# A two-branch decoder step on one core: row sums on TensorE, a first product moved inside PSUM, GpSimd work in pieces

## The chip, the cores and the metric

The kernel runs on one core of a Trainium2 chip. Its time is device time in microseconds (us), the median of several runs on the chip. A core has TensorE (PE) for matrix products, VectorE (DVE), ScalarE (ACT) and GpSimd (POOL) for elementwise work, SyncE (SP) and the DMA queues for transfers. Operands lie in SBUF; TensorE writes its products to PSUM, eight banks of which the other engines read and write.

## The reference

One step of a decoder layer for 1024 prompt rows and 8 sample rows, width 1024, in float32. A mixer comes first, then a squared-ReLU feed-forward block of width 4096:

```python
def trunk(x, c, ...):
    mod = (silu(c) @ w_ada[l] + b_ada[l])[:, None, :]
    sh1, sc1, g1, sh2, sc2, g2 = jnp.split(mod, N_MOD, axis=-1)
    h = rmsnorm(x, norm1_g[l]) * (1 + sc1) + sh1
    y, bp, bs, bc = mixer(h, ...)            # input projection, convolutions, output projection
    x = x + g1 * y
    h = rmsnorm(x, norm2_g[l]) * (1 + sc2) + sh2
    x = x + g2 * (jnp.square(jax.nn.relu(h @ w_ff1[l])) @ w_ff2[l])
    return rmsnorm(x, final_g), ...
```

The change lies in the last of these blocks: the entry to `h @ w_ff1` with the root mean square of x that it needs, and the product with `w_ff2`.

## The kernel before

**Numbers.** A float32 operand is split into a rounded high half and a low half (value minus high half). A product is high by high, high by low and low by high: three matmuls. ScalarE makes high halves (`high_split`, L1043, of weights; `queue_high`, L1109, of hidden tiles), VectorE or GpSimd makes low halves by a subtraction (VectorE: `low_split` L1779 and `queue_low` L1892; GpSimd: `low_split` L825, four blocks of 128x1024 or the last one 128x512).

**Seven products.** The feed-forward weights and the activations are cut in 2x2 blocks and multiplied by a Strassen-Winograd scheme: products p0 to p6 in place of eight. Sums of weight blocks are made by VectorE's `mix_weights` (L1763 to L1769, four additions of 128x512), sums of hidden tiles by `mix_hidden` (L1829 to L1836). While a product's bank in PSUM is still to be read by another engine, TensorE can't start the next product in that bank.

**Up-projection (`h @ w_ff1`).** Sixteen units; each has seven products of 24 matmuls of 128x262 (L2335, from `product_of`, or `up` in unit 0). Bank pairs are `BANK_X[unit % 2]` for p0, p2, p4 and p6, `BANK_Y` for p1 and `BANK_V` for p3 and p5. ScalarE copies three partial results of a unit from PSUM (`copy_c`, L1094), VectorE adds the rest (`add_c`, L1793; `last_c`, L1816), scales by the row norms (`scale_c`), ScalarE applies ReLU and square (`activate`, L1101 and L1104), SyncE stores the hidden tiles to memory (`store_hidden`) and later fetches the queue pieces back.

The norm of x's rows is needed only at `scale_c`. Squares are made in place, a tile of 128x1024 at a time (`square_row`, L1026); VectorE adds rows 0 to 6 onto row 7 (`add_row`, L1842); TensorE sums over the partitions with a column of ones (`hidden_sums`, which calls `token_sums`, L2138, 16 matmuls of one column), and spreads the norm over a bank (`hidden_spread`, L2391 to L2396). All of it lies in units 0 and 1, the entry of the up-projection. Its order is written out by hand, per engine; ScalarE's copy after the squares waits for `rows_summed`.

**Product stage (with `w_ff2`).** Fourteen rounds w of 14 steps. A step is product p of output block jj, 12 matmuls of 128x258 (L2444, `down(w, n)`), in the order of `STEPS`. After each step VectorE's `gather` (L1942 where the sum is touched first, L1945 afterwards) adds the bank pair to the sum in SBUF, and `y_added` counts these additions; a step waits until the addition that read its bank is counted. Between the additions VectorE has, by the round, four `mix_weights` and a number of `queue_low`. ScalarE makes the high halves of the next round's weights and of the next group's queue pieces (two rounds share a group). Four weight blocks a round get their low half from GpSimd. `QUEUE` is the order of the queue pieces. After the last round come `rejoin` and `part`, which finish the output.

```python
STEPS = [(0, 0), (0, 1), (1, 0), (3, 0), (2, 0), (2, 1), (1, 1), (5, 0), (4, 0), (4, 1), (3, 1), (6, 0), (6, 1), (5, 1)]
bank = (BANK_X[jj], BANK_Y, BANK_X[jj], BANK_V, BANK_X[jj], BANK_V, BANK_X[jj])[p]
```

## Time and profile before

| | us |
|---|---|
| median of three runs | 1103.91 (1102.61 to 1107.77) |
| the profiled execution: its own time | 1106.11 |
| span of its profile | 1104.3 |
| TensorE busy | 1038.8 |
| VectorE busy | 902.8 |
| ScalarE busy | 407.5 |
| GpSimd busy | 241.9 |

The profile shows one execution. Times within it are microseconds from the start of the span. A row of a group gives busy time and mean ns of one instruction; idle time before an instruction is put down to the event that ended it last. PEld is TensorE's loading of weights, which runs beside its matmuls. The mean granted TensorE clock was 0.979 of full speed.

### The profile page before, as it was taken

To read this page: it belongs to the slowest core of one execution; us is meant where nothing else is said; L and a number is where in the kernel's file an instruction comes from. 1 tells how busy PE (TensorE), PEld (TensorE's weight loads), DVE (VectorE), ACT (ScalarE), POOL (GpSimd) and SP (SyncE) were. 2 spreads that over 40 slices of the span, in tenths; PEclk is the share of its full clock that TensorE was granted. 3 is DMA by queue.
4 is the path that set the end of the run, shared out by engine and by line. 5 is a ranking of instruction groups with operands and counts; after the bars stand their busy time and mean duration, and the time that the engine had idled before them with its cause. 6 is when DMAs were issued, how large, how long until landed. Compare 5 with 4: busy or idle time off the path is not lost.

```text
span 1104.3 us, 19181 instructions
## 1 busy us (share of the span) xinstructions
PE 1038.8 (94%) x7811; PEld 1003.2 (91%) x7811; DVE 902.8 (82%) x1236; ACT 407.5 (37%) x584; POOL 241.9 (22%) x188
## 2 busy tenths in 40 slices
PE   7899999999999769899999999998999999998896
PEld 5688898999999669799999999988999999998896
DVE  5799899996458986677677677699999999998866
ACT  6321111111233554555555455472333333332221
POOL 2741121221114200000000000033443443443300
PEclk8899999999999989999999999999999999999999
DMA  9967411110113130544534534585554444335212
GB/s 279 352 235 299 138 39 39 39 42 26 48 44 132 77 98 29 188 151 146 165 117 146 174 110 150 184 291 170 148 148 132 144 147 137 98 105 184 78 57 98
DMA packets 112769, 148.62 MB, mean 135 GB/s; under 512 B 6465, under 2 KB 78088, under 8 KB 110617
## 3 DMA queue, kind: packets, MB, share of 16 engines
q1 hardware_dynamic: 111928, 146.15, 41.0%
q8 instruction: 62, 1.02, 0.4%
q0 software_dynamic: 336, 0.58, 0.2%
q10 hardware_dynamic: 417, 0.65, 0.2%
q14 instruction: 26, 0.21, 0.1%
HBM read 110.40 MB, written 37.44 MB: 134 GB/s over the span
## 4 chain that ended last, share of the span: by engine, by line
PE 64%; DVE 21%; issue 9%; DMA 3%; ACT 2%; SPq 1%; DVEq 0%; ACTq 0%
PE banks L2335 25%; PE banks L2107 17%; PE banks L2444 13%; DVE plain L1428 4%; DVE xT L1945 3%; PE banks L2485 3%; DVE split L1892 2%; DMA plain<-hid_home 1%; DVE split L1642 1%; DMA plain<-in_x_prompt 1%; DVE plain L1769 1%; PE banks L2202 1%; PE banks L2224 1%; DVE plain L1447 1%; PE banks L2515 1%
## 5 line engine op out<-in xcount | busy, mean ns | idle before, releaser
L2335 PE MATMUL banks<-split 128*128 128x262 f32 x2688 | 334.2, 287 | 19.3 <-ACT xT L1094 12.1
L2335 PEld LDWEIGHTS banks<-split 128*128 128x128 f32 x2688 | 331.3, 191 | 22.0 <-ACT xT L1094 12.7
L2444 PE MATMUL banks<-split 128*128 128x258 f32 x2352 | 289.3, 285 | 13.0 <-DVE xT L1945 10.9
L2444 PEld LDWEIGHTS banks<-split 128*128 128x128 f32 x2352 | 285.2, 190 | 16.9 <-DVE xT L1945 13.9
L2107 PEld LDWEIGHTS banks<-split 128*128 128x128 f32 x1656 | 265.9, 192 | 12.6 <-issue 7.4
L2107 PE MATMUL banks<-split 128*128 128x344 f32 x1656 | 270.1, 325 | 6.5 <-DVE gate_s L1488 6.0
L825 POOL TENSOR_TENSOR split<-plain,split 128x1024 fp32r<-128x1024 f32 (+1 forms) x59 | 130.3, 2219 | 525.0 <-ACT split L1043 524.9
L1043 ACT ACTIVATE split<-plain 128x1024 fp32r<-128x1024 f32 (+1 forms) x120 | 112.6, 949 | 177.6 <-PE banks L2444 139.4
L1945 DVE TENSOR_TENSOR xT<-xT,banks 128x516 f32<-128x516 f32 x180 | 122.1, 684 | 19.7 <-PE banks L2444 13.8
L1428 DVE SCALAR_TENSOR_TENSOR plain<-plain 128x1023 f32<-128x1023 f32 (+14 forms) x90 | 132.6, 1473 | 2.9
L768 POOL TENSOR_TENSOR split<-plain,split 128x1024 fp32r<-128x1024 f32 (+2 forms) x29 | 64.3, 2218 | 249.0 <-ACT split L876 249.0
L1892 DVE TENSOR_TENSOR split<-plain,split 128x524 fp32r<-128x524 f32 x106 | 113.3, 1074 | 1.1 <-ACT split L1109 1.1
L876 ACT ACTIVATE split<-plain 128x1024 fp32r<-128x1024 f32 (+2 forms) x29 | 27.3, 942 | 210.5 <-PE banks L2107 177.4
L1793 DVE TENSOR_TENSOR xT<-xT,banks 128x524 f32<-128x524 f32 x44 | 30.7, 699 | 54.2 <-PE banks L2335 54.1
L1779 DVE TENSOR_TENSOR split<-plain,split 128x1024 fp32r<-128x1024 f32 (+1 forms) x61 | 66.3, 1087 | 1.9 <-ACT split L1043 1.8
L1109 ACT ACTIVATE split<-plain 128x524 fp32r<-128x524 f32 x106 | 60.5, 628 | 16.8 <-PE banks L2444 12.7
L1101 ACT ACTIVATE xT<-xT 128x516 f32<-128x516 f32 x60 | 43.4, 724 | 49.4 <-DVE xT L1805 49.4
L1094 ACT ACTIVATE xT<-banks 128x524 f32<-128x524 f32 x45 | 27.3, 607 | 69.9 <-PE banks L2335 62.0
L2485 PE MATMUL banks<-split 128*128 128x258 f32 x384 | 49.5, 286 | 3.1 <-DVE gate_s L1999 3.1
L2485 PEld LDWEIGHTS banks<-split 128*128 128x128 f32 x384 | 46.9, 189 | 3.9 <-DVE gate_s L1999 3.9
L1104 ACT ACTIVATE xT<-xT 128x516 f32<-128x516 f32 x60 | 38.2, 637 | 1.9
L1484 DVE SCALAR_TENSOR_TENSOR xT<-banks,modT,xT 128x688 f32<-128x688 f32 x16 | 14.9, 929 | 27.7 <-PE banks L2107 27.7
(233 smaller groups left out, 815.9 us busy)
## 6 DMA issues: line engine op xcount, KB each, us to landing
plain<-hid_home SPq DMA_DIRECT2D x106, 262.0 KB, 3.7
hid_home<-xT SPq DMA_DIRECT2D x102, 262.0 KB, 3.1
plain<-in_w_ff SPq DMA_DIRECT2D x18, 1024.0 KB, 6.6
plain<-in_w_ada SPq DMA_DIRECT2D x16, 1024.0 KB, 7.4
plain<-in_w_ff SPq DMA_DIRECT2D x56, 256.0 KB, 3.7
plain<-in_w_in SPq DMA_DIRECT2D x17, 512.0 KB, 6.2
plain<-in_w_ada SPq DMA_DIRECT2D x16, 512.0 KB, 6.7
plain<-in_x_prompt SPq DMA_DIRECT2D x8, 512.0 KB, 8.2
```

Of the source, the lines that this page charges most:

```text
L768: nc.gpsimd.tensor_tensor(o, a, b, ALU.subtract).then_inc(wlo_ready, 1)
L825: nc.gpsimd.tensor_tensor(split_of(g, 1), split_source(unit, g), split_of(g, 0).bitcast(F32), ALU.subtract).then_inc(split_lo, 1)
L1043: nc.scalar.activation(split_of(g, 0), src, ACT.Copy).then_inc(split_hi, 1)
L1109: nc.scalar.activation(queue_piece(n, 0), stage(n), ACT.Copy).then_inc(queue_hi, 1)
L1428: ins = nc.vector.scalar_tensor_tensor(dc[:, c, s:T], glu[:, c, 0:T - s], tapT[:, tap:tap + 1], dc[:, c, s:T], ALU.mult, ALU.add)
L1779: nc.vector.tensor_tensor(split_of(g, 1), src, split_of(g, 0).bitcast(F32), ALU.subtract).then_inc(split_lo, 1)
L1892: nc.vector.tensor_tensor(queue_piece(n, 1), stage(n), queue_piece(n, 0).bitcast(F32), ALU.subtract).then_inc(queue_lo, 1)
L1945: nc.vector.tensor_tensor(out, out, ps, ALU.add).then_inc(y_added, 1)
L2107: last = nc.tensor.matmul(out[:, t, 0:TW], w[:, slot, b, :], x[:, k, t * TW:(t + 1) * TW], start=(i == 0 and w is whi and x is hi), stop=( ...
L2335: last = nc.tensor.matmul(banks[:, bank + t, 0:width], weight(p, w, i), operand(p, x, pieces[n], t, width), start=(p in FIRST_OF_CHAIN and ...
L2444: last = nc.tensor.matmul(banks[:, bank + t, 0:QT], weight(p, h, 2 * kb + jj), halves(queue_piece(e, x))[:, t, 0:QT], start=(p in FIRST_OF ...
L2485: last = nc.tensor.matmul(banks[:, bank, 0:QT], late_split(j, w)[:, 2 * b + dd, :], src, start=(b == 0 and w == 0 and x == 0), stop=(b == ...
```

## The change

Three edits.

**1. GpSimd in pieces.** Its subtractions of weight low halves (`low_split` and the late ones before the tail) are issued as pieces of 128x512, two where there was one of 128x1024.

**2. Rows 0 and 1 summed by TensorE.** ScalarE squares rows 0 and 1 right after the second weight rounding of unit 0. TensorE sums each over the partitions into a bank that is free then, VectorE reads the result into `sumsq`, scaled, and the norm's formula takes it as an addend. `add_row` has five rows left. In units 0 to 2 the orders of ScalarE and VectorE are written anew; on TensorE `hidden_sums` now stands between p0 and p1 of unit 1 and the two `hidden_spread` after p2 and p3; `mix_hidden(0)` stands ahead of `last_c(1)`.

**3. Product 0 moved inside PSUM.** `STEPS` gets another order. Product 0 of a block is copied by ScalarE from `BANK_X[jj]` to `BANK_Y` (`move`), and product 1 is accumulated onto it, so that VectorE adds 12 bank pairs a round instead of 14. The queue pieces and their halves follow in another order, with some of the first group's made later.

```diff
-STEPS = [(0, 0), (0, 1), (1, 0), (3, 0), (2, 0), (2, 1), (1, 1), (5, 0), (4, 0), (4, 1), (3, 1), (6, 0), (6, 1), (5, 1)]
+STEPS = [(0, 0), (3, 0), (0, 1), (1, 0), (2, 0), (5, 0), (1, 1), (2, 1), (4, 0), (3, 1), (4, 1), (6, 0), (5, 1), (6, 1)]
...
+ADDS = [n for n, (p, _) in enumerate(STEPS) if p]
...
-ROW_SQUARED = {7: 1, 0: 2, 1: 3, 2: 4, 3: 5, 4: 6, 5: 7, 6: 8}
-QUEUE = [(g, p, kb) for g in range(GROUPS) for p in ((0, 1, 2, 3, 4, 5, 6) if g == 0 else (3, 4, 5, 6, 0, 2, 1))
+ROW_SQUARED = {0: 1, 1: 2, 2: 3, 7: 4, 3: 5, 4: 6, 5: 7, 6: 8}
+QUEUE = [(g, p, kb) for g in range(GROUPS) for p in ((0, 1, 2, 3, 4, 5, 6) if g == 0 else (3, 4, 5, 6, 0, 1, 2))
          for kb in range(2)] + [(GROUPS, b, half) for half in range(2) for b in range(FG)]
...
+                out, src, hi = split_of(g, 1), split_source(unit, g), split_of(g, 0).bitcast(F32)
+                for b in range(0, HALF_N[g] // P, 4):
+                    ins = nc.gpsimd.tensor_tensor(out[:, b:b + 4], src[:, b:b + 4], hi[:, b:b + 4], ALU.subtract)
+                ins.then_inc(split_lo, 1)
...
             oper_high(1, 5)
             high_split(0, 1)
+            square_row(0)
+            square_row(1)
...
-            square_row(7)
-            square_row(0)
-            square_row(1)
-            act.wait_ge(rows_summed, 2)
+            act.wait_ge(two_summed, 1)
             copy_c(0, 2, BANK_X[0], 2)
             square_row(2)
             copy_c(0, 1, BANK_V, 3)
+            square_row(7)
+            square_row(3)
             high_split(1, 0)
+            square_row(4)
             high_split(1, 1)
-            square_row(3)
+            square_row(5)
+            square_row(6)
             high_split(1, 2)
-            square_row(4)
-            act.wait_ge(rows_summed, 3)
+            act.wait_ge(rows_summed, 1)
             copy_c(0, 3, BANK_X[0], 6)
             high_split(1, 3)
-            square_row(5)
-            square_row(6)
 
 
             copy_c(1, 0, BANK_X[1], 0)
+            root(3)
             high_split(2, 0)
-            act.wait_ge(rows_summed, 4)
+            act.wait_ge(rows_summed, 2)
             copy_c(1, 2, BANK_X[1], 2)
...
+            def move(w, jj):
+
+                act.wait_ge(product_made, made(UP + 2 * w + jj, 0))
+                if jj:
+                    act.wait_ge(y_added, added_step(w, STEP_AT[1, 0]))
+                elif w:
+                    act.wait_ge(y_added, added_step(w - 1, STEP_AT[1, 1]))
+                else:
+                    act.wait_ge(c_added, added_at(UP - 1, 1))
+                nc.scalar.activation(banks[:, BANK_Y:BANK_Y + 2, 0:QT], banks[:, BANK_X[jj]:BANK_X[jj] + 2, 0:QT],
+                                     ACT.Copy).then_inc(moved, 1)
...
             for g in range(GROUPS):
                 unit, n = UP + 2 * g, 2 * NP * (g + 1)
-                for k in range(4):
-                    queue_high(n + k)
+                move(2 * g, 0)
+                if g:
+                    queue_high(n)
+                    queue_high(n + 1)
+                    queue_high(n + 2)
+                move(2 * g, 1)
+                if g:
+                    queue_high(n + 3)
                 high_split(unit + 1, 0)
-                for k in range(4, 7):
+                for k in range(4 if g else 0, 7 if g else 4):
                     queue_high(n + k)
                 high_split(unit + 1, 1)
-                queue_high(n + 7)
+                if g:
+                    queue_high(n + 7)
                 high_split(unit + 1, 2)
                 high_split(unit + 1, 3)
+                move(2 * g + 1, 0)
+                if g == 0:
+                    queue_high(n + 4)
+                    queue_high(n + 5)
+                    queue_high(n + 6)
...
-            add_row(0, 1)
-            add_row(1, 2)
+            dve.wait_ge(two_summed, 1)
+            nc.vector.tensor_scalar(sumsq[:, 0:KD], banks[:, BANK_X[1] + 1, 0:KD], 1.0 / D, EPS, ALU.mult, ALU.add
+                                    ).then_inc(two_read, 1)
+            add_row(2, 1)
+            add_row(3, 2)
             dve.wait_ge(oper_lo, len(LO_ORDER))
             dve.wait_ge(ext_ready, 3)
             nc.vector.memset(rb[:, :, 0, 256:HT], 1.0).then_inc(rb_ones, 1)
             nc.vector.memset(rb[:, :, 1, 256:258], 1.0).then_inc(rb_ones, 1)
+            add_c(0, 1, BANK_X[0], 4, 2)
+            low_split(1, 0)
+            add_row(4, 3)
             mix_all(1)
-            low_split(1, 0)
-            add_c(0, 1, BANK_X[0], 4, 2)
-            add_row(2, 3)
+            add_c(0, 2, BANK_V, 5, 3)
             low_split(1, 1)
-            add_c(0, 2, BANK_V, 5, 3)
-            add_row(3, 4)
+            add_row(5, 4)
+            add_row(6, 5)
             low_split(1, 2)
-            add_row(4, 5)
             low_split(1, 3)
-            add_row(5, 6)
-            add_row(6, 7)
...
+            dve.wait_ge(sq_used, 2)
+            dve.wait_ge(two_read, 1)
+            link(nc.vector.scalar_tensor_tensor(rstd[:, 0:KD], banks[:, BANK_X[0], 0:KD], 1.0 / D, sumsq[:, 0:KD],
+                                                ALU.mult, ALU.add))
+            nc.vector.tensor_scalar(rstd[0:S, KD:R], banks[0:S, BANK_X[0], KD:R], 1.0 / D, EPS, ALU.mult, ALU.add
+                                    ).then_inc(ms_ready, 1)
+            dve.wait_ge(rows_summed, 5)
+            diagonals(3, diag2)
             add_c(1, 0, BANK_Y, 1, 1)
             mix_all(2)
-            dve.wait_ge(sq_used, 2)
-            mean_squares(3, banks[:, BANK_X[0], :], D)
             low_split(2, 0)
-            dve.wait_ge(rows_summed, 7)
-            diagonals(3, diag2)
-            add_c(1, 1, BANK_X[1], 4, 2)
-            low_split(2, 1)
-            add_c(1, 2, BANK_V, 5, 3)
-            low_split(2, 2)
             dve.wait_ge(rb_ready, 3)
             dve.wait_ge(copied, 4)
             scale_c(0, 0)
             scale_c(0, 1)
             scale_c(0, 2)
+            add_c(1, 1, BANK_X[1], 4, 2)
             scale_c(0, 3)
+            low_split(2, 1)
             scale_c(1, 0)
+            add_c(1, 2, BANK_V, 5, 3)
             scale_c(1, 1)
             scale_c(1, 2)
+            low_split(2, 2)
+            mix_hidden(0)
             last_c(1)
             low_split(2, 3)
-            mix_hidden(0)
...
-                    gather(w, k)
+                    if STEPS[k][0]:
+                        gather(w, k)
...
-                        if k < 2:
-                            queue_low(12 + k)
-                        elif k < 4:
-                            queue_low(n + k - 2)
-                        else:
-                            queue_low(n + k - 6)
+                        queue_low(8 + k if k < 4 else 4 + k)
+                    elif w == 1:
+                        queue_low(n + (4 + k if k < 4 else k))
...
+            pe.wait_ge(row_squared, 2)
+            token_sums(banks[:, x1 + 1, :], xT[:, 0, :], True, False)
+            token_sums(banks[:, x1 + 1, :], xT[:, 1, :], False, True).then_inc(two_summed, 1)
...
+                if unit == 1:
+                    pe.wait_ge(two_read, 1)
                 if unit > 1:
                     pe.wait_ge(c_added, added_at(unit - 2, 4))
                     if unit == 2:
                         pe.wait_ge(rb_ready, 3)
                 product_of(0, x, every, both, every, HT).then_inc(product_made, 1)
+                if unit == 1:
+                    hidden_sums()
                 pe.wait_ge(c_added, added_at(unit - 1, 1))
                 product_of(1, BANK_Y, every, both, every, HT).then_inc(product_made, 1)
-                if unit == 1:
-                    hidden_sums()
                 pe.wait_ge(copied, ahead + 1)
                 pe.wait_ge(split_lo, split_at(unit, 1))
                 product_of(2, x, every, both, every, HT).then_inc(product_made, 1)
+                if unit == 1:
+                    hidden_spread(True)
                 pe.wait_ge(c_added, added_at(unit - 1, 3))
                 product_of(3, BANK_V, every, both, every, HT).then_inc(product_made, 1)
+                if unit == 1:
+                    hidden_spread(False)
                 pe.wait_ge(copied, ahead + 2)
                 pe.wait_ge(split_lo, split_at(unit, 2))
                 product_of(4, x, every, both, every, HT).then_inc(product_made, 1)
-                if unit == 1:
-                    hidden_spread(True)
                 pe.wait_ge(copied, ahead + 3)
                 product_of(5, BANK_V, every, both, every, HT).then_inc(product_made, 1)
-                if unit == 1:
-                    hidden_spread(False)
...
-                                                    start=(p in FIRST_OF_CHAIN and kb == 0 and h == 0 and x == 0),
+                                                    start=(p in (0, 3) and kb == 0 and h == 0 and x == 0),
...
-                    if w or before_step[n] >= 0:
-                        pe.wait_ge(y_added, step(w, before_step[n]))
-                    elif bank_of[n] < 2:
-                        pe.wait_ge(c_added, added_at(UP - 2 + n, 4))
+                    (p, jj), earlier = STEPS[n], before_step[n]
+                    if p == 1 or (p == 2 and earlier >= 0):
+                        pe.wait_ge(moved, 2 * w + jj + 1)
+                    elif earlier >= 0:
+                        pe.wait_ge(y_added, added_step(w, earlier))
+                    elif w:
+                        pe.wait_ge(y_added, added_step(w - 1, earlier + 2 * NP))
+                    elif p == 0:
+                        pe.wait_ge(c_added, added_at(UP - 2 + jj, 4))
                     else:
-                        pe.wait_ge(c_added, added_at(UP - 1, (1, 3)[bank_of[n] - 2]))
+                        pe.wait_ge(c_added, added_at(UP - 1, 3))
                     down(w, n)
```

**The rows on ScalarE.** The first place is ScalarE's queue at the entry, units 0 and 1. `xT` is x, `plain` holds raw weights and partial results, `split` the rounded halves; 128x524 are the copies of partial results. Before:

```order
L1094 ACTIVATE plain<-banks 128x524
L1001 ACTIVATE split<-xT,A 128x2x256
L1001 ACTIVATE split<-plain 128x2x256 x2
L1026 ACTIVATE xT<-xT 128x1024 x3
L1094 ACTIVATE xT<-banks 128x524
L1026 ACTIVATE xT<-xT 128x1024
L1094 ACTIVATE xT<-banks 128x524
L1043 ACTIVATE split<-plain 128x1024 x2
L1026 ACTIVATE xT<-xT 128x1024
```

After (L1108 is `copy_c`, L1013 `oper_high`, L1038 `square_row`, L1055 `high_split`):

```order
L1108 ACTIVATE plain<-banks 128x524
L1013 ACTIVATE split<-xT,A 128x2x256
L1013 ACTIVATE split<-plain 128x2x256 x2
L1108 ACTIVATE xT<-banks 128x524
L1038 ACTIVATE xT<-xT 128x1024
L1108 ACTIVATE xT<-banks 128x524
L1038 ACTIVATE xT<-xT 128x1024 x2
```

Two squares (rows 0 and 1) stand earlier in the same queue, behind a weight rounding of unit 0:

```order
L1013 ACTIVATE split<-plain 128x2x256 x3
L1055 ACTIVATE split<-plain 128x1024
L1038 ACTIVATE xT<-xT 128x1024 x2
L1013 ACTIVATE split<-xT,A 128x2x256 x3
L1020 ACTIVATE plain<-plain,A 128x512
L1013 ACTIVATE split<-plain 128x2x256
```

Three squares that stood ahead of the copy `copy_c(0, 2, ...)` (the first 128x524 copy into xT) are gone from there; two of them stand earlier, one later.

**The additions on VectorE.** The second place is VectorE's queue at the same point, from the first addition of a partial result (L1793 before, L1821 after) on. Before:

```order
L1793 TENSOR_TENSOR plain<-plain,banks 128x524
L1842 TENSOR_TENSOR xT<-xT 128x1024 x2
L1850 MEMSET misc 128x2x6
L1851 MEMSET misc 128x2x2
L1763 TENSOR_TENSOR plain<-plain 128x512
L1765 TENSOR_TENSOR plain<-plain 128x4x128
L1767 TENSOR_TENSOR plain<-plain 128x512
L1769 TENSOR_TENSOR plain<-plain 128x512
L1779 TENSOR_TENSOR split<-plain,split 128x1024
L1793 TENSOR_TENSOR xT<-xT,banks 128x524
L1842 TENSOR_TENSOR xT<-xT 128x1024
```

After (L1870 is `add_row`, L1807 `low_split`, L1791 to L1797 `mix_weights`):

```order
L1821 TENSOR_TENSOR plain<-plain,banks 128x524
L1875 TENSOR_SCALAR sumsq<-banks 128x8
L1870 TENSOR_TENSOR xT<-xT 128x1024 x2
L1881 MEMSET misc 128x2x6
L1882 MEMSET misc 128x2x2
L1821 TENSOR_TENSOR xT<-xT,banks 128x524
L1807 TENSOR_TENSOR split<-plain,split 128x1024
L1870 TENSOR_TENSOR xT<-xT 128x1024
L1791 TENSOR_TENSOR plain<-plain 128x512
L1793 TENSOR_TENSOR plain<-plain 128x4x128
L1795 TENSOR_TENSOR plain<-plain 128x512
L1797 TENSOR_TENSOR plain<-plain 128x512
L1821 TENSOR_TENSOR xT<-xT,banks 128x524
```

The reading of the two sums is new; the two row additions behind it are those of rows 2 and 3, where they were those of rows 0 and 1, and the addition of the next partial result and a low half have moved ahead of the four weight sums.

**A round on ScalarE.** The third place is ScalarE's queue in the first round of a group in the product stage. Before:

```order
L1109 ACTIVATE split<-plain 128x524 x6
L1043 ACTIVATE split<-plain 128x1024
L1109 ACTIVATE split<-plain 128x524 x3
L1043 ACTIVATE split<-plain 128x1024
L1109 ACTIVATE split<-plain 128x524
L1043 ACTIVATE split<-plain 128x1024
L1043 ACTIVATE split<-plain 128x512
```

After (L1222 is `move`, L1123 `queue_high`):

```order
L1222 ACTIVATE banks<-banks 128x2x258
L1123 ACTIVATE split<-plain 128x524 x3
L1222 ACTIVATE banks<-banks 128x2x258
L1123 ACTIVATE split<-plain 128x524
L1055 ACTIVATE split<-plain 128x1024
L1123 ACTIVATE split<-plain 128x524 x3
L1055 ACTIVATE split<-plain 128x1024
L1123 ACTIVATE split<-plain 128x524
L1055 ACTIVATE split<-plain 128x1024
L1055 ACTIVATE split<-plain 128x512
```

Two copies from PSUM to PSUM stand in each round, the second of them behind three queue pieces and ahead of the rest.

## Rows read from the trace of the kernel before

**Rows 1.** The page's busy times by engine (span 1104.3 us).

```profile
PE 1038.8 (94%) x7811; PEld 1003.2 (91%) x7811; DVE 902.8 (82%) x1236; ACT 407.5 (37%) x584; POOL 241.9 (22%) x188
```

**Rows 2.** Timeline of TensorE, entry: start, length, instructions, idle before and its releaser.

```profile
380.38 5.38 PE L2335 MATMUL banks<-split 128*128 128x262 f32 x42 [2.27 <-DVE split L1675]
...
400.00 16.22 PE L2335 MATMUL banks<-split 128*128 128x262 f32 x120 [7.93 <-ACT xT L1094]
416.06 1.84 PE L2138 MATMUL banks<-ones,xT 128*128 128x1 f32 x16
...
417.95 9.05 PE L2335 MATMUL banks<-split 128*128 128x262 f32 x72
...
450.98 7.53 PE L2335 MATMUL banks<-split 128*128 128x262 f32 x48 [4.16 <-ACT xT L1094]
459.77 10.41 PE L2335 MATMUL banks<-split 128*128 128x262 f32 x83 [1.27 <-DVE xT L1793]
```

**Rows 3.** Timeline of all engines, 335 to 410: ScalarE and VectorE.

```profile
392.09 1.22 DVE L1779 TENSOR_TENSOR split<-plain,split 128x1024 fp32r<-128x1024 f32 x1
...
394.65 2.95 ACT L1026 ACTIVATE xT<-xT 128x1024 f32<-128x1024 f32 x3 [3.75 <-DVE split L1645]
396.76 2.56 DVE L1842 TENSOR_TENSOR xT<-xT 128x1024 f32<-128x1024 f32 x2 [1.58 <-ACT xT L1026]
...
399.34 0.61 ACT L1094 ACTIVATE xT<-banks 128x524 f32<-128x524 f32 x1 [1.74 <-DVE xT L1842]
...
400.00 0.69 DVE L1763 TENSOR_TENSOR plain<-plain 128x512 f32<-128x512 f32 x1 [0.66 <-DMA plain<-in_w_ff]
```

**Rows 4.** Timeline of all engines, 405 to 475: the wait for a store.

```profile
444.04 0.70 DVE L1836 TENSOR_TENSOR xT<-xT 128x524 f32<-128x524 f32 x1
...
450.32 0.61 ACT L1094 ACTIVATE xT<-banks 128x524 f32<-128x524 f32 x1 [6.17 <-DMA hid_home<-xT]
```

**Rows 5.** Windows: stretch, its length, busy time by engine, granted clock, DMA.

```profile
395.00:400.00 5.00, 0.00 (x0) 0.00 (x0) 2.66 (x5) 3.26 (x5) 0.00 (x0) 0.61 0.83 255
400.00:405.00 5.00, 5.00 (x30) 5.00 (x31) 4.38 (x6) 4.35 (x5) 0.00 (x0) 0.71 0.48 165
```

**Rows 6.** Timeline of all engines, 840 to 890: one round of the product stage.

```profile
856.73 0.69 DVE L1892 TENSOR_TENSOR split<-plain,split 128x524 fp32r<-128x524 f32 x1
...
857.76 2.39 POOL L825 TENSOR_TENSOR split<-plain,split 128x1024 fp32r<-128x1024 f32 x1 [3.33 <-ACT split L1043]
857.94 2.77 DVE L1892 TENSOR_TENSOR split<-plain,split 128x524 fp32r<-128x524 f32 x1
...
861.37 20.46 PE L2444 MATMUL banks<-split 128*128 128x258 f32 x168 [0.52 <-DVE xT L1945]
```

**Rows 7.** TensorE's waits: line, releaser, us in total, times, longest.

```profile
PE banks L2444 <- DVE xT L1945: 10.9, 14, 2.0
```

**Rows 8.** Timeline of TensorE, last unit and first round of the product stage.

```profile
727.72 3.19 PE L2335 MATMUL banks<-split 128*128 128x262 f32 x24 [1.43 <-DVE xT L1793]
...
733.27 13.54 PE L2444 MATMUL banks<-split 128*128 128x258 f32 x108 [0.92 <-DVE xT L1816]
...
748.78 6.04 PE L2444 MATMUL banks<-split 128*128 128x258 f32 x48 [1.97 <-DVE xT L1945]
```

**Rows 9.** Timeline of TensorE, end of the product stage.

```profile
1009.03 1.72 PE L2444 MATMUL banks<-split 128*128 128x258 f32 x12 [1.39 <-DVE xT L1945]
...
1012.47 20.51 PE L2444 MATMUL banks<-split 128*128 128x258 f32 x156 [1.71 <-DVE xT L1945]
```

**Rows 10.** Groups by line and shape: busy us, mean ns of one, idle before.

```profile
L1945 DVE TENSOR_TENSOR xT<-xT,banks 128x516 f32<-128x516 f32 x180 | 122.1, 684 | 19.7 <-PE banks L2444 13.8 <-DVE plain L1767 1.6 <-DVE plain L1763 1.0
...
L1109 ACT ACTIVATE split<-plain 128x524 fp32r<-128x524 f32 x106 | 60.5, 628 | 16.8 <-PE banks L2444 12.7 <-DMA plain<-hid_home 4.0
...
L1094 ACT ACTIVATE xT<-banks 128x524 f32<-128x524 f32 x45 | 27.3, 607 | 69.9 <-PE banks L2335 62.0 <-DMA hid_home<-xT 6.2 <-DVE xT L1842 1.7
```

**Rows 11.** Timeline of all engines, 335 to 410: one GpSimd subtraction.

```profile
377.69 1.28 POOL L825 TENSOR_TENSOR split<-plain,split 128x512 fp32r<-128x512 f32 x1 [7.15 <-ACT split L1043]
```

More of the change, by code:

```diff
@@ L495, in decoder_trunk @@
         y_added = sem("y_added")
+        moved = sem("moved")
         x_returned = [sem(f"x_returned{i}") for i in range(4)]
@@ L840, in _ @@
                 src = raw_of(last + j // 2).rearrange("p (f j) m n -> p f j (m n)", f=FG)[:, :, j % 2, :]
-                nc.gpsimd.tensor_tensor(late_split(j, 1).rearrange("p (f m) n -> p f (m n)", f=FG), src,
-                                        late_split(j, 0).bitcast(F32).rearrange("p (f m) n -> p f (m n)", f=FG),
-                                        ALU.subtract).then_inc(split_lo, 1)
+                out = late_split(j, 1).rearrange("p (f m) n -> p f (m n)", f=FG)
+                hi = late_split(j, 0).bitcast(F32).rearrange("p (f m) n -> p f (m n)", f=FG)
+                for f in (0, 2):
+                    ins = nc.gpsimd.tensor_tensor(out[:, f:f + 2], src[:, f:f + 2], hi[:, f:f + 2], ALU.subtract)
+                ins.then_inc(split_lo, 1)
         @block.scalar
@@ L1149, in _ @@
                                  ACT.Copy).then_inc(rb_ready, 1)
-            high_split(2, 2)
+            high_split(2, 1)
             activate(0, 0)
             activate(0, 1)
-            high_split(2, 3)
             activate(0, 2)
-            copy_c(2, 0, BANK_X[0], 0)
             activate(0, 3)
+            high_split(2, 2)
             activate(1, 0)
-            high_split(3, 0)
-            copy_c(2, 2, BANK_X[0], 2)
             activate(1, 1)
             activate(1, 2)
-            copy_c(2, 1, BANK_V, 3)
-            high_split(3, 1)
-            activate(1, 3)
-            activate(2, 0)
-            activate(2, 1)
-            high_split(3, 2)
-            activate(2, 2)
-            high_split(3, 3)
-            for unit in range(3, UP):
+            high_split(2, 3)
+            for unit in range(2, UP):
                 last = unit == UP - 1
@@ L1190, in _ @@
                 activate(unit, 1)
+                high_split(unit + 1, 2)
+                activate(unit, 2)
                 if last:
@@ L1193, in _ @@
                     queue_high(9)
-                high_split(unit + 1, 2)
-                activate(unit, 2)
-                if last:
-                    queue_high(10)
-                    queue_high(11)
                 high_split(unit + 1, 3)
             activate(UP - 1, 3)
-            queue_high(12)
-            queue_high(13)
+            for n in range(10, 14):
+                queue_high(n)
             def late_high(j):
@@ L1903, in _ @@
                 else:
-                    for n in range(6):
+                    for n in range(4):
                         queue_low(n)
```

40 lines of the change are left out of this document (22 added, 18 removed).

## The prediction

> **What bounds the kernel now.** I read the busy shares first: TensorE is busy for 1038.8 of 1104.3 us [rows 1], so all that a change can win is in some 65 us of idle TensorE and in stretches where it runs slowly. The waits of TensorE and then its timeline say where these lie. Most of the idle time falls in three places: the entry to the up-projection, its end, and the product stage (the down-projection). In the entry [rows 2] TensorE stands still for 7.93 us before 400.00, for 4.16 before 450.98 and for 1.27 before 459.77. The first gap is a chain of three rows in [rows 3]: ScalarE squares three rows of x at 394.65, after VectorE's last operand is done; VectorE adds two of them, 2.56 us from 396.76; only then may ScalarE copy the partial result that TensorE waits for (399.34). The second gap is a copy that waited 6.17 us for a store of the hidden tiles [rows 4]. The clock follows: 0.61 of full speed was granted at 395 to 400 and 0.71 at 400 to 405, 30 matmuls in 5 us [rows 5], where 168 take 20.46 at full clock [rows 6]. That is 2.4 GHz, and the loss is about 1.5 us.
>
> In the product stage TensorE waits 14 times, 10.9 us in all, for VectorE adding a finished product to its sum [rows 7]. A round is 14 steps of 12 matmuls, 20.46 us, or 1.46 a step, plus a stall of 0.52 [rows 6]. The stall's cause is in the same group: at 857.76 GpSimd starts a 2.39 us subtraction, and a VectorE subtraction that takes 0.69 a row earlier needs 2.77, to 0.56 after GpSimd's end. The add behind it comes too late by half a microsecond. Stalls at the stage's ends are longer: 1.43, 0.92 and 1.97 at the start [rows 8], 1.39 and 1.71 at the end, where 156 matmuls also took 20.51 instead of 19.0, 1.5 us of slow clock [rows 9].
>
> **Row sums by TensorE, and the new order in the entry.** Rows 0 and 1 are squared and summed on TensorE while it waits 2.27 us for VectorE before 380.38 anyway [rows 2]. The sum is 2 x 16 matmul rows at 1.84 us per 16 [rows 2], 3.7 us, so 1.4 us stick out; they fall into the next wait, which ends with a ScalarE copy, and cost nothing. Without that cover they cost 3.7. The two squares add 2 us to ScalarE (2.95 for three [rows 3]) where it had nothing to do.
>
> The 7.93 us gap then ends with the next condition, the VectorE subtraction at 392.09, 1.22 long [rows 3]: products start at 393.4 instead of 400.0. What is late next? Unit 1's weights, which land at 400.0 as before (VectorE's start there was released by the DMA [rows 3]). From there: ScalarE's rounding, 1.0 (as a square of that size), VectorE's low half 1.22, one row add 1.28, four weight mixes of 0.7 (400.00 in [rows 3]), ScalarE's next rounding 1.0, two squares 2.0, two adds of which one is behind the squares, 1.3 to 1.6: 411.0. TensorE, with three products (24 matmuls, 2.94 each at the pace of [rows 6]) and one more, is at its moved row sum at 405.3. It waits 5.7 us, a new stall, after which I count 1.5 us of slow clock as in [rows 5]. The sum takes 1.9 (416.06 to 417.95 in [rows 2]), the next product 2.94: unit 1's third product starts at 417.3 against 417.95. Of the 7 us only 0.6 is left there.
>
> The rest comes later. The spread of the row norms now follows the third and fourth product instead of the fifth and sixth, 5.9 us earlier, and the mix of unit 0's hidden tiles is put ahead of unit 1's last product. In the old trace that mix ended at 444.74 and the copy went at 450.32, 5.6 us for the stores [rows 4]. It now ends near 438, so the tile is free near 443.6, and TensorE comes to it at 445.2. Old: from 417.95 to the end of unit 2 at 462.7 (459.77 plus a product) is 44.8 us. New: twelve products, 35.3, and two spreads, 1.4: 36.7, so 454.0. **Entry: -8.7.**
>
> **The copies inside PSUM.** Each of 28 removes a VectorE operation of 0.68 [rows 10] and adds a ScalarE copy of 128x516 from PSUM to PSUM. No row of the trace shows ScalarE writing PSUM. The nearest is its copy of 128x524 from PSUM to SBUF, 0.607 [rows 10]; I take 0.6, with bounds 0.45 and 1.2 (twice the row). The Trainium skill, "ScalarE: Activation LUTs", section "Step-by-step: what each stage is for", says that PSUM is the faster destination for ScalarE. By that the copy would be under 0.6, and no run here has shown it yet. The matmul that lands on the copy is two steps (2.9 us) behind its source, so one copy in time costs TensorE nothing. But it stands in ScalarE's queue: the second copy of a round waits for VectorE's add of step 3, and behind it stands the rounding of a queue piece (0.63 [rows 10]), for which VectorE waits in turn. After step 3's end: add 0.9, copy 0.7, rounding 0.7, low half 0.7: VectorE is free again at 3.0. Ahead of it are then 10 adds, 4 mixes and 4 low halves, 18 of about 0.63, 11.4.
>
> **GpSimd in pieces.** A subtraction of 128x512 took 1.28 on its own [rows 11], half of 2.39 being 1.20, so GpSimd loses little. VectorE subtractions now wait for half as long at a time, but after each low half comes an add from PSUM, during which GpSimd takes the next piece, so VectorE's next subtraction waits again. Walking through the round I find five waits between step 3 and the end, 0.5 to 0.9 each, 3.4 together. The last add but one then ends 3.0 + 11.4 + 3.4 - 0.6 = 17.2 after step 3, and the new order of steps needs it at 16.1: (3,0) is now the second step of a round, two steps behind (5,1), where it was three. Stall 1.1. The same walk over the old order gives 0.8 where the row has 0.5, so the new round is 0.3 longer. The Trainium skill, "SBUF — State Buffer", section "Who interferes with whom", says the same of the pair of ports: who comes first holds it for the whole instruction. The trace agrees (2.77 against 0.69). By that rule taken alone, half the instruction is half the wait, the five waits would be near 0.35 each, and the stall would go; that is a rival below.
>
> **Sum of the product stage.** The last unit's 1.43 [rows 8] goes, since two low halves are moved behind the add: -1.4. First round, walked through in the same way: the pieces that (3,0) needs now come later on VectorE and (3,0) itself earlier (2.5), the first copy stands behind a relu and square and four roundings on ScalarE (2.2), and a low half comes late in the round (1.9), 6.6 in all. Against it stand 0.92 and 1.97 of before and 0.6 by which the matmuls behind them took longer than 1.46 a step (13.54 for nine, 6.04 for four [rows 8]): +3.1. Second round: two stalls shorter, -1.4. Ten rounds at +0.3: +3. Last two: 4.6 of stalls and slow clock [rows 9] go, about 1 comes: -3.6. **Stage: -0.3**, with bounds of -12 (no stalls) and +9 (copies of 1.2, or pieces of 1.3).
>
> **Result.** -8.7 - 0.3 = -9.0 against the profiled execution's 1106.11 (span 1104.3, 1.8 around it), 1097.1. That execution is 2.2 above the median of the runs, so against 1103.91 the forecast is **1095 us**.
>
> **Rivals.** (a) *VectorE gets clear*: its five waits stay under 0.45 each, and no round stalls. For it speaks that 12 adds instead of 14 are left; against it, that the alternation of low half and add gives GpSimd every second slot. Ten rounds at -0.8 instead of +0.3: 1095 - 11 = 1084 to 1087. (b) *The product stage gives the entry back*: pieces take 1.3 and copies 0.9, rounds are 0.7 longer, +5 to +8: 1100 to 1104, no change. Also here if the row sum's stall at 405 is 3 us longer. (c) *Slower: copies inside PSUM are slow.* VectorE's chain after step 3 holds the copy, so each us of it above 0.6 stalls one round by one us, 14 times. From 1.6 us on it decides: +14, over 1109; at 1.8, 1112. Nothing in the trace excludes it, but ScalarE operations of this size are at 0.61 and 0.63 [rows 10]. (d) The copies do nothing, since ScalarE's queue was free anyway: the entry alone, 1095; the same time as the forecast.
>
> **How the numbers follow.** This kernel's runs (1102.61 to 1107.77) can tell a difference of about 0.5%, 5.5 us. Forecast with (d): 0.47, of which 0.05 above 1098.4; (a) 0.20; (b) 0.20; (c) 0.13. Faster 0.42 + 0.20 = 0.62, same 0.25, slower 0.13. The range reaches to (a) and through (b): 1084 to 1106, leaving out (c) and a little below (a). The forecast alone is 1091 to 1099.
>
> **What would show it.** In the profile after: no gap before unit 0's fifth product (at 393.4, not 400), a new one of 5 to 6 us before the row sum near 405, no wait for a store near 450, unit 3 beginning near 454. ScalarE's PSUM copies at 0.6. Product rounds of 21.0 to 21.4 with the stall at a round's first and second step. Wrong if rounds are 20.2 (a), if the copies are above 1 us (c), or if the row sum does not wait.

## The result, and the profile after

The changed kernel takes 1097.89 us (median of eight runs, 1095.81 to 1100.73) against 1104.21: a ratio of 0.9944, interval 0.9927 to 0.9961, 6.3 us less. Beside the experiments it was measured once more: 1096.52 against 1105.40, 0.9915 (0.9887 to 0.9944), 8.9 less. The forecast was 1095, 9 less. The profiled execution took 1097.58 with a span of 1095.8.

The busy times of the page, beside [rows 1]: VectorE does 29 operations fewer (28 copies or additions of product 0 and one more), ScalarE 28 more.

```profile
PE 1047.4 (96%) x7843; PEld 1010.6 (92%) x7843; DVE 873.4 (80%) x1207; ACT 425.9 (39%) x612; POOL 269.1 (25%) x236
```

GpSimd is busy for 27 us more with the same data: a piece takes 1.28 alone [rows 11], and 1.52 on average here. In the groups by shape the PSUM copy is there, at 585 ns (columns as in [rows 10]):

```profile
L1222 ACT ACTIVATE banks<-banks 128x516 f32<-128x516 f32 x28 | 16.4, 585 | 53.6 <-DVE xT L1975 34.9 <-PE banks L2477 13.2 <-DVE xT L1972 5.5
```

TensorE's timeline in the entry and in the product stage, to be held against [rows 2], [rows 6] and [rows 9]:

```profile
377.14 5.84 PE L2166 MATMUL banks<-ones,xT 128*128 128x1 f32 x32
382.84 21.25 PE L2363 MATMUL banks<-split 128*128 128x262 f32 x150
404.25 3.19 PE L2363 MATMUL banks<-split 128*128 128x262 f32 x24 [0.15 <-DVE split L1807]
413.22 3.55 PE L2166 MATMUL banks<-ones,xT 128*128 128x1 f32 x16 [5.78 <-DVE xT L1870]
...
416.82 8.66 PE L2363 MATMUL banks<-split 128*128 128x262 f32 x48
...
429.79 55.45 PE L2363 MATMUL banks<-split 128*128 128x262 f32 x450
...
725.71 1.61 PE L2477 MATMUL banks<-split 128*128 128x258 f32 x12
...
772.94 21.15 PE L2477 MATMUL banks<-split 128*128 128x258 f32 x168 [0.43 <-DVE xT L1975]
...
1007.39 19.02 PE L2477 MATMUL banks<-split 128*128 128x258 f32 x156 [0.43 <-DVE xT L1975]
1026.25 7.39 PE L2523 MATMUL banks<-split 128*128 128x258 f32 x60
```

The gap of 7.93 before unit 0's fifth product is gone, and so are the waits of 4.16 and 1.27 behind it: from 429.79 on TensorE runs through. In their place stands one gap of 5.78 before the row sum of unit 1. In the product stage every round from the third on now has a stall of 0.38 to 0.44 at its second step; from 772.94 to 1007.39 eleven rounds take 21.31 each.

The windows of the same entry (columns as in [rows 5]) show TensorE's clock at its lower level twice: right behind the 32 one-column matmuls, and behind the gap and the 16 others.

```profile
380.00:385.00 5.00, 5.00 (x24) 5.00 (x25) 4.82 (x8) 3.33 (x6) 0.00 (x0) 0.50 0.00 0
385.00:390.00 5.00, 5.00 (x30) 5.00 (x30) 3.53 (x6) 1.05 (x4) 0.00 (x0) 0.66 0.00 0
...
410.00:415.00 5.00, 1.78 (x9) 1.81 (x9) 4.71 (x5) 4.91 (x7) 0.00 (x0) 0.73 0.01 3
415.00:420.00 5.00, 5.00 (x25) 4.96 (x25) 2.12 (x7) 0.21 (x1) 0.00 (x0) 0.50 0.69 210
420.00:425.00 5.00, 5.00 (x34) 5.00 (x33) 2.43 (x4) 1.06 (x1) 0.00 (x0) 0.74 0.00 0
```

One product round of the timeline, VectorE, ScalarE and GpSimd:

```profile
859.15 1.53 DVE L1925 TENSOR_TENSOR split<-plain,split 128x524 fp32r<-128x524 f32 x1 [0.23 <-ACT split L1123]
...
863.79 0.58 ACT L1222 ACTIVATE banks<-banks 128x516 f32<-128x516 f32 x1 [3.61 <-DVE xT L1975]
864.28 0.63 ACT L1123 ACTIVATE split<-plain 128x524 fp32r<-128x524 f32 x1
864.95 0.70 DVE L1925 TENSOR_TENSOR split<-plain,split 128x524 fp32r<-128x524 f32 x1 [1.26 <-ACT split L1123]
...
868.51 3.00 POOL L835 TENSOR_TENSOR split<-plain,split 128x512 fp32r<-128x512 f32 x2 [8.39 <-ACT split L1055]
868.83 1.53 DVE L1795 TENSOR_TENSOR plain<-plain 128x512 f32<-128x512 f32 x1
...
871.00 1.06 DVE L1797 TENSOR_TENSOR plain<-plain 128x512 f32<-128x512 f32 x1
...
873.80 1.37 DVE L1925 TENSOR_TENSOR split<-plain,split 128x524 fp32r<-128x524 f32 x1
...
875.70 1.19 DVE L1925 TENSOR_TENSOR split<-plain,split 128x524 fp32r<-128x524 f32 x1
...
877.41 1.57 DVE L1925 TENSOR_TENSOR split<-plain,split 128x524 fp32r<-128x524 f32 x1
```

Operations of 0.68 to 0.70 take 1.06 to 1.57 five times between 868 and 879: 3.3 us of waiting behind GpSimd. (The subtraction at 859.15 waits too; it lies ahead of step 3 of the round.) At 864.95 VectorE stands still for 1.26: it waits for the rounding at 864.28, which stands behind the second PSUM copy in ScalarE's queue.

### The profile page after: what moved, and what is told of

It reads as the page before. It is cut to its first block, busy times and chain, and to the rows that moved or that the text cites. A ratio compares the mean times of both kernels' runs of the same rounds, so it can differ in the third digit from the quotient of the medians.

```text
span 1095.8 us, 19294 instructions
## 1 busy us (share of the span) xinstructions
PE 1047.4 (96%) x7843; PEld 1010.6 (92%) x7843; DVE 873.4 (80%) x1207; ACT 425.9 (39%) x612; POOL 269.1 (25%) x236
## 4 chain that ended last, share of the span: by engine, by line
PE 62%; DVE 26%; issue 7%; SPq 2%; ACT 2%; DMA 1%; DVEq 0%; ACTq 0%
PE banks L2363 27%; PE banks L2135 17%; PE banks L2477 8%; DVE xT L1975 6%; PE banks L2523 4%; DVE plain L1456 4%; DVE split L1925 3%; DVE plain L1795 2%; SPq L577 1%; DVE plain L1797 1%; PE banks L2166 1%; DVE split L1670 1%; DVE plain L1793 1%; ACT split L1123 1%; DVE plain L1791 1%
## 5 line engine op out<-in xcount | busy, mean ns | idle before, releaser
L835 POOL TENSOR_TENSOR split<-plain,split 128x512 fp32r<-128x512 f32 x103 | 153.6, 1515 | 498.2 <-ACT split L1055 498.2
L1055 ACT ACTIVATE split<-plain 128x1024 fp32r<-128x1024 f32 (+1 forms) x120 | 114.1, 951 | 121.7 <-PE banks L2477 60.0
L1456 DVE SCALAR_TENSOR_TENSOR plain<-plain 128x1023 f32<-128x1023 f32 (+14 forms) x90 | 136.3, 1514 | 2.9
L776 POOL TENSOR_TENSOR split<-plain,split 128x1024 fp32r<-128x1024 f32 (+2 forms) x29 | 66.8, 2303 | 247.7 <-ACT split L888 226.9
L1925 DVE TENSOR_TENSOR split<-plain,split 128x524 fp32r<-128x524 f32 x106 | 105.9, 1009 | 24.8 <-ACT split L1123 24.8
L1975 DVE TENSOR_TENSOR xT<-xT,banks 128x516 f32<-128x516 f32 x152 | 103.1, 684 | 16.5 <-PE banks L2477 15.3
L1821 DVE TENSOR_TENSOR xT<-xT,banks 128x524 f32<-128x524 f32 x44 | 30.8, 699 | 54.6 <-PE banks L2363 54.6
L1807 DVE TENSOR_TENSOR split<-plain,split 128x1024 fp32r<-128x1024 f32 (+1 forms) x61 | 66.2, 1087 | 3.2 <-ACT split L1055 3.2
L1123 ACT ACTIVATE split<-plain 128x524 fp32r<-128x524 f32 x106 | 61.7, 630 | 17.8 <-PE banks L2477 15.2
L1108 ACT ACTIVATE xT<-banks 128x524 f32<-128x524 f32 x45 | 27.3, 607 | 66.5 <-PE banks L2363 64.0
```

The source lines that it names most:

```text
L776: nc.gpsimd.tensor_tensor(o, a, b, ALU.subtract).then_inc(wlo_ready, 1)
L835: ins = nc.gpsimd.tensor_tensor(out[:, b:b + 4], src[:, b:b + 4], hi[:, b:b + 4], ALU.subtract)
L1055: nc.scalar.activation(split_of(g, 0), src, ACT.Copy).then_inc(split_hi, 1)
L1123: nc.scalar.activation(queue_piece(n, 0), stage(n), ACT.Copy).then_inc(queue_hi, 1)
L1456: ins = nc.vector.scalar_tensor_tensor(dc[:, c, s:T], glu[:, c, 0:T - s], tapT[:, tap:tap + 1], dc[:, c, s:T], ALU.mult, ALU.add)
L1807: nc.vector.tensor_tensor(split_of(g, 1), src, split_of(g, 0).bitcast(F32), ALU.subtract).then_inc(split_lo, 1)
```

## The experiments

**Each part by itself.** `entry_only` is the kernel before with edit 2, `product_only` with edits 1 and 3; `after_again` is the changed kernel. Each is made of whole pieces of the diff above, of which these are the cores (first `entry_only`, then `product_only`):

```diff
             high_split(0, 1)
+            square_row(0)
+            square_row(1)
...
-            add_row(0, 1)
-            add_row(1, 2)
+            dve.wait_ge(two_summed, 1)
```

```diff
+                move(2 * g, 0)
...
-                    gather(w, k)
+                    if STEPS[k][0]:
+                        gather(w, k)
```

> The kernel before with edit 2 alone (rows 0 and 1 summed by TensorE, new order of the entry); the product stage is that of before. By the trace of the changed kernel unit 2 ends 3.4 us earlier than before (last_c of unit 3 at 480.15 against 483.50), although the forecast had 8.7: if that is all the entry gives, the time is 3 to 4 us under before, 1100 to 1101. Rival, the forecast's own sum: the entry is worth 8.7 and the product stage gave nothing, 1095 to 1096.

> The kernel before with edits 1 and 3 alone (pieces, copies inside PSUM, new steps); the entry is that of before, with its gap of 7.9 us before unit 0's fifth product. By the two traces the product stage and the tail take 3.4 us less and the last unit 1.4 less: 1099 to 1100. Rival, the forecast's sum: 0 to 1 us less than before, 1103 to 1104.

> The changed kernel once more, to stand beside the two parts. Theory: the parts add up, 8.6 us for the entry alone and 1.7 for the product stage alone, so it lies 10 us under before, at a ratio of 0.990 to 0.992. Rival: one part takes 2 to 4 us from the other, and the ratio is 0.993 to 0.996, as in its first runs.

The entry alone: 1096.79 against 1105.42, ratio 0.9914 (0.9900 to 0.9929), 8.6 less. The product stage alone: 1103.77, 0.9982 (0.9972 to 0.9992), 1.7 less. Both times the forecast's own sum, my rival, came out nearer than the reading of the two traces. Together they should give 10.3; the second measurement of the changed kernel gives 8.9, the first 6.3, and the intervals hold 10.3 in the second and not in the first, so a small loss between the parts is neither shown nor excluded.

Why one pair of traces misled: the entry differs from execution to execution. Unit 3's last VectorE step shows how late a kernel leaves the entry; these are the first trace of before, its second and that of the change:

```profile
483.50 0.70 DVE L1816 TENSOR_TENSOR xT<-banks,misc 128x524 f32<-128x524 f32 x1 [0.15 <-PE banks L2335]
...
488.73 0.70 DVE L1816 TENSOR_TENSOR xT<-banks,misc 128x524 f32<-128x524 f32 x1
...
480.15 0.70 DVE L1844 TENSOR_TENSOR xT<-banks,misc 128x524 f32<-128x524 f32 x1
```

And the end of the product stage in the first trace held stalls that a second profile does not show:

**The kernel before, once more** (`before_again`, no edit).

> The kernel before, profiled once more. In its first trace the last round of the product stage had two stalls of 1.4 and 1.7 us and 1.5 us of slow matmuls; in the trace of the entry edit alone, whose product stage is the same code, they are missing. Theory: they belong to that kernel's timing (when the last queue pieces land) and stand in its second trace too. Rival: a chance event of one execution; then the last rounds are clean and the profiled time is 3 to 5 us lower.

It took 1106.86. The rival was right about the stalls and wrong about the time, since its entry was longer. TensorE's timeline:

```profile
735.98 1.59 PE L2444 MATMUL banks<-split 128*128 128x258 f32 x12
...
782.68 20.46 PE L2444 MATMUL banks<-split 128*128 128x258 f32 x168 [0.52 <-DVE xT L1942]
...
1013.31 20.45 PE L2444 MATMUL banks<-split 128*128 128x258 f32 x168 [0.52 <-DVE xT L1945]
1033.60 4.48 PE L2485 MATMUL banks<-split 128*128 128x258 f32 x36
```

The last round runs in 20.45 with the usual stall, where [rows 9] has 1.39, 1.71 and slow matmuls (granted clock 0.77 at 1015 to 1020). In the first trace each of these two stalls stands behind a VectorE subtraction that started just behind a whole GpSimd one and took 2.90 (at 1005.48 and 1008.90). How often an execution of before has them was not measured: of its two profiles one has, and `entry_only`, with the same product stage, has not.

**With and without pieces.** `no_pieces` is the changed kernel without edit 1, `pieces_only` the kernel before with edit 1 alone, `entry_pieces` with edits 1 and 2, so without the PSUM copies and the new steps.

```diff
-                nc.gpsimd.tensor_tensor(split_of(g, 1), split_source(unit, g), split_of(g, 0).bitcast(F32),
-                                        ALU.subtract).then_inc(split_lo, 1)
+                out, src, hi = split_of(g, 1), split_source(unit, g), split_of(g, 0).bitcast(F32)
+                for b in range(0, HALF_N[g] // P, 4):
+                    ins = nc.gpsimd.tensor_tensor(out[:, b:b + 4], src[:, b:b + 4], hi[:, b:b + 4], ALU.subtract)
+                ins.then_inc(split_lo, 1)
...
```

> The changed kernel without edit 1: GpSimd's subtractions are 128x1024 again. Theory: a VectorE operation that starts behind GpSimd waits to GpSimd's end, so whole subtractions make waits of up to 2.1 us in place of 0.4 to 0.9, and the product rounds of 21.3 get 0.3 to 1 us longer: 1101 to 1109. Rival: the number of waits counts and not their length, since pieces give GpSimd every second slot; then rounds get shorter by up to 0.8 and the time is 1088 to 1096.

> The kernel before with edit 1 alone. Theory: in the old order of steps VectorE's one long wait of 2.1 behind GpSimd makes the stall of 0.5 a round; halves of it make two short waits of less sum, so the stall goes: 12 rounds of 0.5, and the stalls of the last rounds, 5 to 10 us less, 1095 to 1100. Rival: pieces make more waits, the sum is the same, 1103 to 1107.

> The kernel before with edits 1 and 2, without edit 3: no copies inside PSUM, the old steps, VectorE adding product 0. Theory: pieces alone gave 12.6 us and the entry alone 8.6, in different stretches, so they add up to 21: 1083 to 1086, as fast as the changed kernel with the rounding put first. Rival: edit 3 is needed for the last stalls once the entry is shorter; 1088 to 1092.

Without pieces: 1128.03, ratio 1.0200 (1.0182 to 1.0218), 22.6 slower than before and some 31 slower than with them (22.6 and the 8.9 of `after_again`), far beyond the theory's 4 to 11. One round of it:

```profile
858.54 2.40 POOL L833 TENSOR_TENSOR split<-plain,split 128x1024 fp32r<-128x1024 f32 x1 [9.68 <-ACT split L1051]
858.84 2.65 DVE L1791 TENSOR_TENSOR plain<-plain 128x512 f32<-128x512 f32 x1
...
862.27 4.63 PE L2473 MATMUL banks<-split 128*128 128x258 f32 x36 [0.65 <-DVE xT L1971]
...
864.56 2.47 DVE L1921 TENSOR_TENSOR split<-plain,split 128x524 fp32r<-128x524 f32 x1
...
868.77 2.32 DVE L1921 TENSOR_TENSOR split<-plain,split 128x524 fp32r<-128x524 f32 x1
```

Each of three whole subtractions now catches a VectorE operation at its start and holds it for 1.6 to 2.0 us, and each makes a stall of TensorE of its own (0.65 at 862.27, then 0.78 and 0.91). A round takes 23.34 us (862.27 to 885.61), where the changed kernel has 21.31.

Pieces alone: 1092.40, ratio 0.9886 (0.9857 to 0.9914), 13.6 less than before by the medians (12.6 by the ratio), and 4.1 and 5.5 us under the two medians of the whole change. Its interval lies below that of the change's first measurement and overlaps that of the second. TensorE's timeline and, in the round, VectorE:

```profile
749.74 268.09 PE L2448 MATMUL banks<-split 128*128 128x258 f32 x2232 [1.23 <-DVE xT L1949]
```

```profile
874.53 1.19 DVE L1896 TENSOR_TENSOR split<-plain,split 128x524 fp32r<-128x524 f32 x1
875.64 0.68 DVE L1949 TENSOR_TENSOR xT<-xT,banks 128x516 f32<-128x516 f32 x1
876.74 0.69 DVE L1949 TENSOR_TENSOR xT<-xT,banks 128x516 f32<-128x516 f32 x1 [0.42 <-PE banks L2448]
```

From 749.74 to the end of the stage TensorE has no stall left, and 168 matmuls take 20.2 us: the round is 0.8 shorter than before's 20.97, of which only 0.52 showed as idle time; at the end of a round VectorE even waits for TensorE, with 14 additions to do. Behind GpSimd its operations stand for up to 0.5 (1.19 against 0.69). With the entry added (`entry_pieces`) it is 1084.62, ratio 0.9815 (0.9787 to 0.9843), 20.8 less: the two add up within the interval. Edits 1 and 3 together gave 1.7 where edit 1 alone gives 13.6, so edit 3 as written costs about 12. `entry_pieces` against `after_again`, measured beside each other, says the same: 1084.62 against 1096.52.

**The rounding ahead of the second copy.** `high_first` is the changed kernel with this, in both rounds of a group:

```diff
-                move(2 * g, 1)
                 if g:
                     queue_high(n + 3)
+                move(2 * g, 1)
```

> The changed kernel with one queue rounding of ScalarE put ahead of the second PSUM copy of a round instead of behind it (rounds 2 to 13). Theory: VectorE has no slack in a round and stands 1.26 us waiting for this rounding; without that wait the stalls of 0.4 and the small ones around it go, rounds fall from 21.3 to 20.5 to 20.8, and 12 rounds give 6 to 9 us: 1089 to 1092. Rival: the waits behind GpSimd set the round and take the time back: 1096 to 1098.

1085.46 against 1105.42, ratio 0.9816 (0.9802 to 0.9830), 20 less than before and 11 to 12 less than the changed kernel: more than the theory's 6 to 9. Its timeline of TensorE, and of the place in the round:

```profile
773.98 241.30 PE L2478 MATMUL banks<-split 128*128 128x258 f32 x2004 [0.45 <-DVE xT L1976]
```

```profile
860.31 0.69 DVE L1926 TENSOR_TENSOR split<-plain,split 128x524 fp32r<-128x524 f32 x1
860.48 0.58 ACT L1222 ACTIVATE banks<-banks 128x516 f32<-128x516 f32 x1 [2.47 <-DVE xT L1976]
861.03 0.69 DVE L1976 TENSOR_TENSOR xT<-xT,banks 128x516 f32<-128x516 f32 x1
```

VectorE's wait of 1.26 at this place is gone, and all stalls behind 773.98 with it. So the cost of edit 3 was not the copy's 0.585 us but what stood behind it in ScalarE's queue. Even so it is only level with `entry_pieces`, which has no copies.

**The gap before the row sum.** `warm` fills the 5.8 us with 36 matmuls of 128x262 whose results are overwritten; `high_warm` does so on top of `high_first`. `sum_later` puts the sum one product later.

```diff
                 if unit == 1:
+                    pe.wait_ge(c_added, added_at(0, 1))
...
+                                        nc.tensor.matmul(banks[:, BANK_Y + t, 0:HT], weight(0, w, i),
+                                                         operand(0, x_, i, t, HT), start=True, stop=True,
...
                     hidden_sums()
```

> The changed kernel with 36 matmuls of 128x262 more, whose results are overwritten, in the 5.8 us that TensorE waits for the row sum of unit 1. Theory: the slow stretch behind that wait (granted clock 0.50 to 0.74 at 415 to 425) comes from TensorE's standing still; with the gap filled the clock stays at 1.00, the 16 one-column matmuls take 1.8 instead of 3.6, the next two products 5.9 instead of 8.7, and the time falls by 4 to 4.5: 1093 to 1094. Rival: the clock falls through the one-column matmuls themselves, as at 380 to 390, and the time stays at 1097 to 1098.

> The changed kernel with the queue rounding ahead of the second copy and with the 36 filling matmuls in the row sum's wait. Theory: both gains stand, the filling worth 2 to 3 us of clock: 1082 to 1084. Rival: the filling alone is worth nothing that can be told, 1085 to 1087.

> The changed kernel with unit 1's row sum behind its second product instead of its first, and the two spreads one product later. Theory: TensorE's wait for VectorE's last row addition shrinks from 5.8 to 2.9, and less slow clock follows: 3 to 6 us less, 1092 to 1095. Rival: the norm comes later, the hidden tiles of unit 0 are stored later, and the wait for that store before unit 2's fifth product is back: 1097 to 1100.

`warm` took 1096.52, 0.9920 (0.9897 to 0.9944), not told apart from the changed kernel. In TensorE's timeline the gap has shrunk to 1.39 and the row sum takes 1.92, but the products behind it still 7.61 where 48 take 5.91 at full speed (450 in 55.45 above), at a clock of 0.83 and 0.82:

```profile
409.76 4.53 PE L2448 MATMUL banks<-split 128*128 128x262 f32 x36
415.68 1.92 PE L2166 MATMUL banks<-ones,xT 128*128 128x1 f32 x16 [1.39 <-DVE xT L1870]
...
417.65 7.61 PE L2363 MATMUL banks<-split 128*128 128x262 f32 x48
```

```profile
415.00:420.00 5.00, 4.32 (x31) 4.31 (x32) 4.06 (x10) 2.58 (x5) 0.00 (x0) 0.83 0.38 98
420.00:425.00 5.00, 5.00 (x37) 5.00 (x36) 2.85 (x5) 1.06 (x1) 0.00 (x0) 0.82 0.32 112
```

`high_warm`, at 1083.63, 0.9810 (0.9783 to 0.9838), can't be told from `high_first`. So the theory that standing still lowers the clock there, and that filling most of the gap keeps it up, has not held. 1.39 us of standing still are left, though, and the one-column matmuls remain as a second cause: neither is shown by itself.

`sum_later` took 1097.19, 0.9928 (0.9903 to 0.9952), no gain either. The gap is half as long, and two new waits stand behind it; the last is for a copy by ScalarE that by its code waits for a store of the hidden tiles, as the rival had it. (The profile names nothing that released this copy from its own wait of 2.68, so the store is inferred.)

```profile
415.55 3.55 PE L2166 MATMUL banks<-ones,xT 128*128 128x1 f32 x16 [2.84 <-DVE xT L1870]
...
436.66 15.03 PE L2363 MATMUL banks<-split 128*128 128x262 f32 x120 [0.92 <-DVE xT L1821]
452.23 32.94 PE L2363 MATMUL banks<-split 128*128 128x262 f32 x268 [0.55 <-ACT xT L1108]
```

## Why the prediction was right, step by step

**The entry, -8.7.** Measured alone it is -8.6, and this agreement is in part luck. The steps are in the trace as forecast: no gap before unit 0's fifth product, a new gap of 5.78 (forecast 5.7), no wait of TensorE near 450. Two sizes were off. The whole chain to the row sum is 2.2 later than 411.0: ScalarE's rounding of unit 1's weights was released by the transfer at 401.81, not at 400.0. And the slow clock behind the gap costs more than the 1.5 us I took: the sum takes 3.47 (413.22 to 416.69) where I had 1.9, the next two products 8.66 instead of 5.88, 4.4 in all. So unit 3 starts near 459.5, not at 454, and against the first trace of before, from which the sum was worked out, the entry gives 3.4 (480.15 against 483.50). The kernel before loses more in other executions than in that trace. In its second trace the matmuls behind its own gap ran slowly, 17.64 and 10.56 us where [rows 2] has 16.22 and 9.05:

```profile
401.53 17.64 PE L2335 MATMUL banks<-split 128*128 128x262 f32 x120 [7.28 <-ACT xT L1094]
...
420.91 10.56 PE L2335 MATMUL banks<-split 128*128 128x262 f32 x72
```

Over all profiles, unit 3's last VectorE step starts at 483.50 to 488.73 in the four with the old entry (`pieces_only` 485.31, `product_only` 485.77) and at 477.96 to 481.39 in the six with the new one as it is in the change. The means are 5.9 apart. So the profiles show some 6 of the 8.6 us; where the rest lies stays open.

**The product stage, -0.3.** Measured alone it is -1.7. By its terms, against the second trace of before: the last unit's 1.43 is gone, as forecast. The first two rounds (725.71 to 772.94, less stall and one step, 45.3, against 735.98 to 782.68, 46.2) are 0.8 shorter, where I had +3.1 and -1.4; in the profile of `after_again` they take 46.3, so this is no more than executions differ by. A round is 0.35 longer (21.31 against 20.97), where I had 0.3: eleven of them are +3.8. The last two rounds give nothing, where I had -3.6: **this term failed**, since I took the stalls of one execution for the kernel's habit. The tail gives 1.9 that I had not counted: TensorE's stretch from the first `part` matmul to its last matmul shrinks from 65.4 to 63.5, start to start. It is 63.9 in `pieces_only` and 64.0 in `no_pieces`, so edits 1 and 3 each give most of it alone. -1.4 - 0.8 + 3.8 - 1.9 is -0.3, the forecast's number by other terms: +1.7 for the first two rounds and -3.6 for the last two were both wrong, and with the tail, left out, the errors cancel. That this number came out is luck; what held is the last unit's term and the longer round.

**The copies.** 0.585 us against 0.6 taken; rival (c) is out, and so is (b), which wanted copies of 0.9 and rounds 0.7 longer. The Trainium skill, "ScalarE: Activation LUTs", section "Step-by-step: what each stage is for", calls PSUM the faster destination. The trace agrees, by little once the size is taken off: 585 ns for 128x516 to PSUM against 607 for 128x524 to SBUF. What I said of the queue behind the copy (the rounding for which VectorE waits in turn) is what `high_first` removed, and it was worth 11 to 12 us, all that kept rival (a) from coming true. The forecast had this wait in its walk through the round, but laid the stall to the waits behind GpSimd. In `high_first` VectorE still waits behind GpSimd (1.19 against 0.69, three times at 867 to 873), and no round stalls. Rival (d), that the copies do nothing, has the time of the entry alone right (1096.79) and the reason wrong: pieces gain and edit 3 loses about as much.

**The pieces.** Five waits of 3.4 together were forecast, five of 3.3 are there. But I costed them only inside the new round. By themselves, in the old order, they take away every stall of a round (13.6 us in all), which the argument never asked. With whole subtractions VectorE is held for 2.1 us in the old order ([rows 6]) and 1.6 to 2.0 in the new, with halves for up to 0.5 in the old order and 0.4 to 0.9 in the new, and the time differs by 13.6 us in the old order and some 31 in the new. The Trainium skill, "SBUF — State Buffer", section "Who interferes with whom", has the rule that whoever comes first holds the pair of ports for the whole instruction. `no_pieces` and `pieces_only` agree with it. By the rule taken alone no round would stall; so it is with pieces in the old order, and in the new one once the rounding is put first.

## What to carry to other kernels

Before a copy is moved to an idle engine, look at what stands behind it in that engine's queue and who waits for that; here one rounding put ahead of the copy was worth more than the whole change. Cost each edit alone in the old order as well as inside the whole: the smallest edit (GpSimd's subtraction in halves) alone was worth at least as much as all three together, and the largest was not needed. A stall that stands once in one trace is no term of a sum until a second execution shows it.

## What the hardware showed that I had not expected

Behind 32 one-column matmuls the granted clock was 0.50 and 0.66 for ten us (380 to 390 after), although TensorE's records are busy there for 5.00 of 5.00 us; the sums took 5.84 us in this execution and 3.63 in that of `entry_only`, with 0.88 and 0.78. The kernel before, without these sums, shows 0.53 at 380 to 385 in its second trace, behind a wait of 2.28, and 1.00 in its first, behind one of 2.27. So the one-column matmuls are not the only way to it. In the same second trace the clock was 0.66 at 420 to 425, behind 16 one-column matmuls with no wait ahead of them, and 1.00 there in the first. Which share is theirs stays open.
